# Output projection and router in one program, with the router's logits made a token tile at a time

## What is computed

```python
x = x + merged @ w_out                       # 512 x 1024, the second output projection
h = rmsnorm_2(x, g_ffn)                      # rows scaled by 1/rms, then a gain per feature
group_logits  = h @ w_grp                    # 512 x 4
expert_logits = h @ w_exp                    # 512 x 32
# best group of 4, in it the best 2 of its 8 experts, weights by softmax
x = x + sum over the chosen experts e: weight_e * (silu(h @ w1[e]) * (h @ w3[e])) @ w2[e]
h = rmsnorm_2(x, g_ple)
x = x + sigmoid(h @ w_pg) * (p @ w_ple)      # the "early products" below are p @ w_ple
```

## Time and profile before

| | |
|---|---|
| median of 3 runs | 1799.13 us (1798.45 to 1801.8) |
| profiled execution | 1799.04 us |
| its span, first to last instruction | 1797.3 us |
| TensorE busy, share of the span | 1691.2 us, 94% |
| VectorE busy | 805.1 us, 45% |
| ScalarE busy | 544.2 us, 30% |
| mean granted TensorE clock | 0.985 |
| bytes moved | 351.76 MB, mean 196 GB/s |

### The profile page before, as it was taken

How to read it: one execution, slowest core, us unless ns; L and a number is a source line. 1 busy time by engine, 2 the same in 40 slices (tenths; PEclk the granted TensorE clock), 3 DMA queues, 4 the chain that set the end, 5 groups by cost and what they waited for, 6 DMA issues and landing times. The chain is left out here.

```text
span 1797.3 us, 20148 instructions
## 1 busy us (share of the span) xinstructions
PE 1691.2 (94%) x8185; PEld 1175.5 (65%) x8185; DVE 805.1 (45%) x1245; ACT 544.2 (30%) x899; POOL 49.8 (3%) x89
## 2 busy tenths in 40 slices
PE   4999999889989999999999999998999988888898
PEld 3888756568878888888788876766343433333456
DVE  6673567654632223365622464244332323232345
ACT  5112366633362222232533450423100000000036
POOL 0000011000000000000000000000200000000000
PEclk9999999989999999999999999999999999999999
DMA  9865210011723332211422021247899999999971
GB/s 374 269 256 162 94 71 1 2 55 64 238 71 103 104 94 94 105 71 48 164 94 94 1 94 48 97 168 305 311 427 424 426 426 425 426 426 425 426 299 48
DMA packets 87400, 351.76 MB, mean 196 GB/s; under 512 B 8246, under 2 KB 39650, under 8 KB 70921
## 3 DMA queue, kind: packets, MB, share of 16 engines
q1 hardware_dynamic: 84418, 346.02, 49.5%
q0 software_dynamic: 2560, 4.37, 0.7%
q10 hardware_dynamic: 328, 0.06, 0.0%
HBM read 346.03 MB, written 8.43 MB: 197 GB/s over the span
## 5 line engine op out<-in xcount | busy, mean ns | idle before, releaser
L594 DVE TENSOR_TENSOR arena<-ring,arena 128x1024 fp32r<-128x1024 f32 x120 | 146.8, 1225 | 229.6 <-ACT arena L651 206.5
L2989 PE MATMUL ex_h<-ring,u_big_tail 128*64 128x512 f32 x544 | 162.1, 610 | 12.6 <-DMA ring<-in_w 6.7
L599 PE MATMUL up_ps<-h_high,arena 128*128 128x512 f32 x352 | 138.1, 392 | 2.9 <-DVE arena L594 2.9
L601 PE MATMUL up_ps<-h_high,arena 128*128 128x512 f32 x352 | 137.5, 391 | 0.0
L600 PE MATMUL up_ps<-arena 128*128 128x512 f32 x352 | 137.4, 390 | 0.0
L651 ACT CAST arena<-ring 128x1024 fp32r<-128x1024 f32 x81 | 84.8, 1047 | 149.5 <-PE up_ps L601 82.2
L2989 PE MATMUL ex_h<-s_ab,u_big_tail 128*64 128x512 f32 x304 | 121.4, 596 | 1.5 <-DVE u_big_tail L2960 1.5
L2989 PEld LDWEIGHTS ex_h<-ring,u_big_tail 128*64 128x64 f32 x544 | 49.7, 139 | 83.2 <-issue 82.1
L2960 DVE TENSOR_TENSOR u_big_tail<-ex_x,vcol 128x512 f32<-128x512 f32 x32 | 20.6, 686 | 177.9 <-PE ex_x L2953 177.9
L3312 ACT ACTIVATE u_big_tail<-ex_h 128x512 f32<-128x512 f32 x16 | 9.6, 598 | 281.2 <-PE ex_h L2989 281.2
L599 PEld LDWEIGHTS up_ps<-h_high,arena 128*128 128x128 f32 x352 | 66.4, 189 | 18.6 <-DVE arena L594 3.3
(11 more groups left out here) (609 smaller groups left out, 3658.5 us busy)
## 6 DMA issues: line engine op xcount, KB each, us to landing
ring<-in_w SPq DMA_DIRECT2D x40, 2048.0 KB, 31.7
s_ab<-in_w SPq DMA_DIRECT2D x32, 2048.0 KB, 32.0
ring<-in_w_in SPq DMA_DIRECT2D x18, 2048.0 KB, 8.5
ring<-in_w_ada SPq DMA_DIRECT2D x24, 1024.0 KB, 7.0
reg_a<-in_w SPq DMA_DIRECT2D x10, 2048.0 KB, 31.9
w1flat<-in_w SPq DMA_DIRECT2D x10, 2048.0 KB, 33.0
ring<-in_w_ffn_gate SPq DMA_DIRECT2D x11, 1024.0 KB, 5.7
ring<-in_w_ffn_up SPq DMA_DIRECT2D x11, 1024.0 KB, 8.3
```

The lines of the kernel that those rows point to most:

```text
L594: return engine.tensor_tensor(lo, v, hi.bitcast(F32), ALU.subtract)
L599: nc.tensor.matmul(ps, x[0], y[0], start=start, stop=False)
L601: return nc.tensor.matmul(ps, x[1], y[0], start=False, stop=stop)
L2989: mm = nc.tensor.matmul(ps[half, :], xT[:, k, half], ws[j][:, k, cols], start=(k == 0), stop=(k == k_end - 1))
```

## The change

The boundary between the output projection and the router is taken out, so both are one program with the experts. In `stage_rows_out` each tile gets its own logits as soon as its features are evicted: `score(t)` takes the tile's features as the stationary operand and the 36 columns of `b.wr` as the moving one, so that the result has tokens on partitions and needs no turning. All four go to one bank, `ps[0]`. TensorE's order becomes turn(1), score(0), turn(2), score(1), turn(3), score(2), score(3). The wide matmul, its copy, `join` and the matmuls with it are gone.

The saves of tiles 2 and 3 move behind the loads of `p` and `w_ple`, and these behind the projection's last product. Load 6 now waits for the logits, as load 7 did. GpSimd's tables start once the fourth tile's rows are made. The clearing of old semaphores, which was done between the programs, is now done by GpSimd alone behind its tables (`retire`), and the other engines wait for it (`retired_again`) at the start of the experts.

```diff
-    if kind == "mod":
+    if kind in ("mod", "rows"):
         b.finished = list(b.passing)
...
-                for t in range(NT):
+                for t in range(2):
                     sp.wait_ge(made, t + 1)
-                    sp.dma_start(b.rows_dram[t * P:(t + 1) * P, :], y[t]).then_inc(b.rows_saved[max(t - 1, 0)], 16)
+                    sp.dma_start(b.rows_dram[t * P:(t + 1) * P, :], y[t]).then_inc(b.rows_saved[0], 16)
...
-            for t in range(2, NT):
-                turn(t)
+
+            def score(t):
+
+                pe.wait_ge(ev_d, t + 1)
+                pe.wait_ge(hi, t + 1)
+                for k in range(KD):
+                    mm = nc.tensor.matmul(ps[0][:, t * NE:(t + 1) * NE], hT[:, k, t * P:t * P + P], b.wr[:, k, 0:NE],
+                                          start=(k == 0), stop=(k == KD - 1))
+                return mm
+            pe.wait_ge(b.wr_in, 32)
+            score(0)
+            turn(2)
+            score(1)
+            turn(3)
+            score(2)
+            score(3).then_inc(b.logits, 1)
...
-    b.end_program()
-    if kind == "rows":
-        b.arena_open.close()
-        b.open_tail()
+    b.arena_open.close()
+    b.open_tail()
...
         @block.sync
         def _(sp):
+            sp.wait_ge(b.rows_ready, 2 * NT)
             sp.dma_start(prow, a["p_2"][0, 0].rearrange("(t p) n -> p t n", p=P)).then_inc(p_in, 16)
             sp.dma_start(b.ple_w, feature_tiles(a["w_ple_2"][0], 0, D)).then_inc(p_in, 16)
+            for t in range(2, NT):
+                sp.wait_ge(b.rows_made, t + 1)
+                sp.dma_start(b.rows_dram[t * P:(t + 1) * P, :], rows[t]).then_inc(b.rows_saved[t - 1], 16)
             sp.wait_ge(b.rows_saved[0], 32)
             sp.wait_ge(b.rows_saved[1], 16)
             sp.wait_ge(b.rows_saved[2], 16)
+            sp.wait_ge(b.logits, 1)
             load_expert(b, sp, 6)
             sp.wait_ge(pool, 10)
             sp.dma_start(b.tok_dram.rearrange("(b s) o -> b (s o)", s=P), zeros[0:SLOTS // P, :]).then_inc(zero, 16)
-            sp.wait_ge(logits, 1)
             load_expert(b, sp, 7)
...
+            g.wait_ge(b.rows_made, NT)
             iota(io32, [[1, EXPERTS]])
...
-            iota(b.io16, [[1, SPILL]])
+            g.wait_ge(b.rows_saved[0], 32)
+            b.retire(g, b.finished)
+            nc.gpsimd.iota(b.io16, pattern=[[1, SPILL]], base=0, channel_multiplier=0,
+                           allow_small_or_imprecise_dtypes=True).then_inc(b.retired_again, 1)
...
         def _(pe):
-            pe.wait_ge(b.wr_in, 32)
-            for k in range(KD):
-                half = slice(64 * (k % 2), 64 * (k % 2) + 64)
-                mm = nc.tensor.matmul(ps_l[half, :], b.wr[:, k, :], b.hT[:, k, :], start=(k < 2), stop=(k >= KD - 2))
-            mm.then_inc(logits, 1)
-            pe.wait_ge(joined, 1)
-            pe.wait_ge(lg_out, 1)
-            for t in range(NT):
-                mm = nc.tensor.matmul(ps_lt[:, t * NE:(t + 1) * NE], lgT[:, t * P:t * P + P], join, start=True, stop=True)
-            mm.then_inc(turned_in, 1)
             pe.wait_ge(p_in, 32)
...
-            nc.vector.tensor_tensor(join, b.ident[:, 0:NE], b.ident[:, 64:64 + NE], ALU.add).then_inc(joined, 1)
-            dve.wait_ge(logits, 1)
-            nc.vector.tensor_copy(lgT, ps_l[:]).then_inc(lg_out, 1)
+            dve.wait_ge(b.logits, 1)
+            link(nc.vector.tensor_copy(lg, b.logit_bank[:, 0:NT * NE].rearrange("p (t n) -> p t n", t=NT)))
             dve.wait_ge(pool, 10)
-            dve.wait_ge(turned_in, 1)
-            link(nc.vector.tensor_copy(lg, ps_lt[:, 0:NT * NE].rearrange("p (t n) -> p t n", t=NT)))
...
# at the start of the experts, on each of SyncE, TensorE, VectorE and ScalarE (here TensorE):
+            pe.wait_ge(b.retired_again, 1)
+            nc.tensor.sem_inc(b.passed, 1)
```

More of the change, by code:

```diff
@@ L190, in lasting_sem, with retire @@
         return self.nc.alloc_semaphore(name=name)
-    def retire(self, pool, old):
+    def retire(self, pool, old, done=None):
         for s in old:
@@ L196, in retire @@
         self.nc.clear_and_free_semaphores(old)
-        self.nc.gpsimd.sem_inc(self.retired, 1)
+        if done is not None:
+            self.nc.gpsimd.sem_inc(done, 1)
     def fresh_sems(self):
@@ L1801, in stage_rows_out @@
         b.wr_clear = b.sem("wr_clear")
+        b.logits, b.rows_ready, b.rows_made = b.lasting_sem("ro_logits"), ready, made
+        NE = EGROUPS + EXPERTS
     with ExitStack() as ps_ctx:
@@ L1804, in stage_rows_out @@
         block = b.block
+        b.logit_bank = ps[0]
         def turn_bank(t, k):
@@ L2683, in stage_router @@
     NE = EGROUPS + EXPERTS
-    lgT, lg, tg, ohg = short.take(T), short.take(NT, NE), short.take(NT, EGROUPS), short.take(NT, EGROUPS)
+    _, lg, tg, ohg = short.take(T), short.take(NT, NE), short.take(NT, EGROUPS), short.take(NT, EGROUPS)
     eg, sel, both, tt = short.take(NT, EGROUPS), short.take(NT, EXPERTS), short.take(NT + 1, EXPERTS), short.take(2 * NT, EXPERTS)
     (mg, pg, m1, m2, e2, r2, s1), at_rank = (short.take(NT) for _ in range(7)), short.take(2 * NT)
-    before, join, zeros, io64 = short.take(P), short.take(NE), short.take(2 * P), short.take(CAP)
+    before, zeros, io64 = short.take(P), short.take(2 * P), short.take(CAP)
     by_rank = short.take(2 * NT, CAP)
@@ L2696, in stage_router @@
     io32, oh = b.io32, b.oh
+    rows = [b.s_ab[:, (8 + 2 * t) * U:(10 + 2 * t) * U] for t in range(NT)]
     oh1, oh2 = oh[:, 0:NT, :], oh[:, NT:2 * NT, :]
@@ L2699, in stage_router @@
     listed = b.listed = b.sem("ro_listed")
-    logits, joined, turned_in, lg_out, chain, expin, expd, ranks, masks, zero, lists, placed, p_in, p_turned, p_moved = (
-        b.sem(f"ro_{n}") for n in ("logits", "joined", "tlogits", "lgout", "chain", "expin", "expd", "ranks", "masks", "zero",
+    chain, expin, expd, ranks, masks, zero, lists, placed, p_in, p_turned, p_moved = (
+        b.sem(f"ro_{n}") for n in ("chain", "expin", "expd", "ranks", "masks", "zero",
                                    "lists", "placed", "pin", "pturn", "pmoved"))
@@ L2705, in stage_router @@
     with ExitStack() as ps_ctx:
-        ps_l, ps_lt, ps_r, ps_t = (ps_ctx.enter_context(nc.psum_tensor(f"ro_{n}", [P, CH], F32)) for n in ("l", "lt", "r", "t"))
+        _, _, ps_r, ps_t = (ps_ctx.enter_context(nc.psum_tensor(f"ro_{n}", [P, CH], F32)) for n in ("l", "lt", "r", "t"))
         ps_p = [ps_ctx.enter_context(nc.psum_tensor(f"ro_p{i}", [P, CH], F32)) for i in range(4)]
@@ L3065, in _ @@
         def _(sp):
+            sp.wait_ge(b.retired_again, 1)
+            nc.sync.sem_inc(b.passed, 1)
             for i in range(4, 2 * NT):
@@ L3092, in _ @@
             nc.gpsimd.memset(fin.eps, EPS).then_inc(fin.eps_in, 1)
+            for i, n in enumerate((32, 16, 16)):
+                pool.wait_ge(b.rows_saved[i], n)
             pool.wait_ge(b.listed, 1)
@@ L3237, in link @@
                 dve.wait_ge(chain, n[0])
+            dve.wait_ge(b.retired_again, 1)
+            nc.vector.sem_inc(b.passed, 1)
             dve.wait_ge(b.list_zero, 16)
             x_in(0)
-            dve.wait_ge(b.tables, 12)
+            dve.wait_ge(b.tables, 11)
             spill_slots(b, dve, link, slots_)
@@ L3298, in _ @@
         def _(act):
+            act.wait_ge(b.retired_again, 1)
+            nc.scalar.sem_inc(b.passed, 1)
             for i in range(4, 2 * NT):
```

3 lines of the change are left out of this document (2 added, 1 removed).

## The result

The changed kernel took 1803.96 us (median of 12 runs, 1801.74 to 1806.2), the kernel before 1799.2 in the same comparison. The ratio is 1.0029, interval 1.0021 to 1.0037: slower by 5 us where 5 us less were forecast. The profiled execution took 1806.2 us, its span is 1804.4, which is 7.1 us over that of the kernel before; the medians are 4.8 us apart.

The account below looks back on a forecast made before the run. Bound: the full DMA stretch, its start set by the router's chain. Old steps of 10.3 us against 5.5 us of new work sticking out gave 4.8 us: 1799.04 - 4.8 = 1794.2, beside the median 1794.3; range 1792.0 to 1799.0.

Parts of the forecast that it names:

- They land near 1245. ... Cover 3 us.: SyncE's queue: saves of tiles 2 and 3, behind 1.5 MB (3.7 us), land before load 6 asks at 1248.5.
- load 7 beyond 1250: Sign of a wrong forecast: SyncE holds load 7 beyond 1250 us; it was expected some 2 us earlier than 1251.29.
- load 8 moved while the end didn't: Sign of a wrong forecast: load 8 moves (1272.64 to 1267.8 us was forecast) but the kernel's end doesn't.
- What they move is the pair's 4 MB into a free queue, off the path: Loads 6 (1.6 us later) and 7 (2 us earlier), needed only after 1295 us, were costed at nothing.
- Should move the start of the full stretch, and with it the end, by the same microsecond: Router chain, 1238 to 1273 us: each microsecond taken out brings full DMA and the end equally earlier; 4.8 us forecast.
- (A): Rival: the clock falls in the router's scores; early 1801.9 us, chance 0.09; late 1798.3 us, chance 0.14.
- (B): Rival: the full DMA queue eats the gain, its start not set by TensorE; 1799.1 or 1800.7 us, chance 0.07.
- (C): Rival: four hand-overs between scores, transposes and evictions cost 0.3 to 0.6 us each; gain 3, 1796.3 us, chance 0.10.
- the gate projection, which the prediction counted for that section: First block's 24-column matmuls, busy without a pause, then clock 0.52: cited as agreeing with the skill's low-clock rule, for (A).

Follow-up runs that it names:

- before, thin products: Kernel before, two programs kept, router's logits made by 64 products of 36 columns, plus 17 semaphore increments per expert pair 5 to 12: 1807.27 us, ratio 1.0052.
- after, scores late: Kernel after with 17 semaphore increments per expert pair 5 to 12, all four tiles' scores behind the last turn: 1799.61 us, ratio 1.0004.
- after, with 17: Kernel after plus 17 semaphore increments on TensorE's queue in each of expert pairs 5 to 12: 1795.26 us, ratio 0.9979; repeated, 1797.14 us, 0.9987.
- before, with 26: Kernel before plus 26 semaphore increments on TensorE's queue in each of expert pairs 5 to 12: 1797.22 us, ratio 0.9989.
- before, load 6 held: Kernel before with load 6 held back to wait for the logits, one line added: 1798.73 us, ratio 1.0002.
- after, saves first: Kernel after, 17 increments per pair, saves of tiles 2 and 3 ahead of the PLE loads, load 6 waiting for saves alone: 1797.86 us, ratio 0.9991.
- after, load 7 late: Kernel after, 17 increments per pair, load 7 moved behind the eight saves of products, just ahead of load 8: 1793.86 us, ratio 0.9979.

## Why the prediction was wrong

**Right, with their sizes.** Scores 0.115 us apart; logits 5.2 us earlier from tile 1, said 4.8; no pause at the boundary; the clock at 1.00 up to 1268 us; the range clear, the tables and the dropped `join` cost nothing; load 8 at 1268.39, 5.1 us earlier from tile 1.

**"They land near 1245. ... Cover 3 us."** This failed first. The 1.5 MB were costed at 3.7 us from 1238.2, which leaves some 3 us for the saves. The last save landed near 1250.3, which is 1249.4 in the times of the trace before: 4 us later than said, 7.6 us after its issue. Load 6 was 2.7 us late from tile 1 instead of 1.6 and load 7 0.9 us early instead of 2, and two of the prediction's own signs of being wrong were there: load 7 beyond 1250 (1251.27), and load 8 moved while the end didn't.

**"What they move is the pair's 4 MB into a free queue, off the path"** is the step that failed in the middle of the kernel. The queue was free when the loads started and not when the first gather did. The list came 4.5 us earlier from tile 1 (22.4 against 26.9), the gather took 4.6 us longer, and at the lower clock the 32 products took 1.7 more. Moving the gather earlier while the loads stand still is the same as moving the loads into it.

**"Should move the start of the full stretch, and with it the end, by the same microsecond"**: this is true in one direction. The delays passed on: in the kernel with thin products in the router's program, 9.4 us late at loads 9 and 10, the branch came 9.3 us late, and with the scores late 3.0 us became 3.9 (beside the kernel after with 17). Gains did not. From tile 1, in us:

| kernel | gather issued | landed after | loads 9, 10 | branch | GB/s in 65 us |
|---|---|---|---|---|---|
| before | 26.9 | 4.5 | 42.9 | 487.6 | 291 |
| before, with 26 | 27.4 | 4.6 | 43.4 | 488.3 | 287 |
| before, load 6 held | 26.9 | 5.1 | 43.0 | 488.6 | 289 |
| before, thin products | 36.3 | 4.5 | 52.4 | 496.9 | 238 |
| after | 22.4 | 9.1 | 43.8 | 487.8 | 290 |
| after, with 17 | 22.4 | 8.1 | 43.0 | 486.8 | 296 |
| after, saves first | 27.6 | 5.0 | 43.0 | 487.8 | 293 |
| after, scores late | 30.5 | 4.9 | 46.0 | 490.7 | 275 |
| after, load 7 late | 24.1 | 4.9 | 39.5 | 488.0 | 301 |

The last column is from the table by stretch, from 4 us ahead of tile 1 for 65 us; before, after, and after with 17:

```profile
1234.16:1299.16 65.00, 55.20 (x265) 26.78 (x265) 28.30 (x96) 16.22 (x38) 13.46 (x25) 0.95 0.78 291
```
```profile
1235.02:1300.02 65.00, 59.29 (x317) 32.65 (x317) 27.55 (x94) 16.92 (x39) 13.50 (x25) 0.95 0.79 290
```
```profile
1234.84:1299.84 65.00, 60.28 (x321) 32.62 (x321) 27.58 (x94) 16.92 (x39) 13.49 (x25) 0.95 0.80 296
```

The stretch behind it is full in all of them (1.01 and 424 to 425 GB/s over the next 419 us), so the bytes that are moved before it should decide: before and after have the same (65 us x 291 and 290 GB/s are 18.9 MB). With thin products it is 3.4 MB less, 8.1 us at 0.425 MB per us, and 9.3 were lost. The kernel with load 7 late is the exception: it moved 0.65 MB more than the kernel before, 1.5 us, and gained nothing; why is open, so the rule is borne out by the delays and not shown for gains.

**The rivals.** (A), the clock, did not come in the scores, and the two kernels with the scores in one row show that it was real. With the scores late the logits came 5.5 us later; 3.3 of them are the clock (10.72 us against 64 x 0.115), the rest is that the turns' pauses stood empty. In these traces tile by tile between the turns kept the clock up during the scores; right behind them it held in six traces and fell in one (load 7 late), so there the margin is thin. (B), given 0.07, came nearest for the middle of the kernel: TensorE still started loads 9 and 10, but the gather and the queue's own work decided when it could. Its price, 1799.1, is where the middle alone ends in the two traces. (C) did not come: the scores and turns ended 0.4 us sooner than summed.

**Not in the forecast at all**: the branch. The step "and with it the end, by the same microsecond" put everything behind the full stretch at no change, without a row for it. The runs showed 5.7 us in the branch itself and 2.5 in the matmuls behind it (9.56 against 7.09) beside a well placed kernel, and 6.0 us from the branch to the end beside the kernel before. It is the whole of the loss, and more: the medians are 4.8 us apart. Lined up equally, the change is worth about 1 us, from ratios of 0.9979 and 0.9987 against 0.9989, whose intervals overlap, so it is not clear of noise; the traces have 1.5 us (486.8 against 488.3).

## What to carry to other kernels

Before believing a difference of a few microseconds, look in both traces at every taken branch and at TensorE's idle time put down to "issue"; a change that adds instructions to a long stream moves every later branch against the fetch blocks, and some 50 to 200 harmless instructions, tried at more than one number, tell whether that is the effect. When a chain that ends in a gather is made shorter, ask what else is in the queues at the new time. Here neither earlier loads nor a later one gave a gain clear of noise, since each brought a new wait, so look for that wait first. Behind a queue that is full to the end the delays counted in full, and no gain did.

## What the runs showed of the hardware

A taken branch on TensorE's queue with 351 instructions to jump took 0.40 to 0.47 us where its target's block had been fetched and 6.06 to 6.18 us where not, with the DMA queues 0.98 busy. The fetches counted ahead of it fit a queue that is one block of 256 instructions ahead and no more. Whether it is shorter with the queues idle was not tried.

With 36 moving columns the clock was at 1.00 in groups of 16, 16 and 32 matmul instructions between transposes, fell in a row of 64 (0.56 over 12 us), and was at 0.50 for all 64 behind a pause of 2.9 us. The Trainium skill (TensorE: Matmul & The Clock Gate, HAM oscillation) puts such falls down to idle gaps between bursts; that agrees with the second case, while the row of 64 fell with only the turns' gaps of 0.8 us ahead of it. Nor does the gate projection, which the prediction counted for that section, bear it out: TensorE was busy without a pause ahead of its fall and 3.29 of 3.41 us in it.
